# Raw modulation weights in a second buffer, and the pooling and convolution work of VectorE at other places in the mixer rounds

## What is computed

```python
def trunk_layer(x, cond, st, ...):
    mod = (jax.nn.silu(cond) @ ada_w + ada_b).astype(x.dtype).reshape(cond.shape[0], N_MOD, 1, D_MODEL)
    sh1, sc1, gt1, sh2, sc2, gt2 = [mod[:, i] for i in range(N_MOD)]
    h = rms_norm(x, norm_g[0]) * (1 + sc1) + sh1
    y, st = mixer_sublayer(h, st, w_in, ...)
    x = x + gt1 * rms_norm(y, norm_g[1])
    h = rms_norm(x, norm_g[2]) * (1 + sc2) + sh2
    a = dwconv_centred(h @ ffn_up, ffn_conv)
    val, gate = jnp.split(a, 2, axis=-1)
    y = (jax.nn.silu(gate) * val) @ ffn_down
    x = x + gt2 * rms_norm(y, norm_g[3])
    return x, st

def mixer_sublayer(h, st, w_in, ...):
    z = h @ w_in                       # q, k, v, o, gates g, gu, gv, pz, cb, cc, cx
    h_a, new_st = bi_mlstm(heads(q), heads(k) * (MLSTM_DH ** -0.5), heads(v), gates, st)
    y_a = jax.nn.sigmoid(o) * h_a
    y_b = chunk_spatial_gate(gu, gv, gmlp_ws, gmlp_b)
    y_c = multiscale_pool(pz, pool_w, pool_scale)
    y_d = cb * dwconv_centred(cc * cx, conv_w)
    return jnp.concatenate([y_a, y_b, y_c, y_d], axis=-1) @ w_out, new_st
```

## Time and profile before

| | before |
|---|---|
| median of 3 runs (lowest to highest) | 829.67 us (828.95 to 832.6) |
| the profiled execution, its own time | 826.83 us |
| its span, first to last instruction | 825.0 us |
| mean granted TensorE clock | 0.972 |
| busy: TensorE / VectorE / ScalarE / GpSimd | 765.9 / 470.8 / 315.6 / 85.8 us |

### The profile page before, as it was taken

One profiled execution on the slowest core, in us unless ns is written; L12 is line 12 of the kernel. 1 busy time (PEld: TensorE's weight loads), 2 busy tenths in 40 slices (PEclk: granted clock), 3 DMA queues, 4 the chain that ended last, 5 costly groups with the idle time before them and its releaser, 6 DMA issues.

```text
span 825.0 us, 12596 instructions
## 1 busy us (share of the span) xinstructions
PE 765.9 (93%) x4754; PEld 692.8 (84%) x4754; DVE 470.8 (57%) x743; ACT 315.6 (38%) x520; POOL 85.8 (10%) x125
## 2 busy tenths in 40 slices
PE   4799999979977998799999999999999999999996
PEld 2489898868866686599999999999999987878785
DVE  2651455755645559765564655555555656756754
ACT  5541422111112247753444335343433333326442
POOL 7600023121200261200000000000000000000000
PEclk9899999989988999899999999999999999999998
DMA  9953108464435854442222222213131235533561
GB/s 301 352 139 106 52 18 240 120 174 134 154 127 204 249 172 130 130 123 77 77 76 76 74 79 76 76 51 102 52 101 51 95 109 169 187 129 124 200 220 68
DMA packets 99534, 107.21 MB, mean 130 GB/s; under 512 B 7000, under 2 KB 79864, under 8 KB 99368
## 3 DMA queue, kind: packets, MB, share of 16 engines
q1 hardware_dynamic: 94007, 94.79, 37.1%
q0 software_dynamic: 3632, 10.20, 4.2%
q10 hardware_dynamic: 1856, 1.71, 0.7%
HBM read 103.89 MB, written 2.80 MB: 129 GB/s over the span
## 4 chain that ended last, share of the span: by engine, by line
PE 80%; DVE 8%; issue 4%; DMA 3%; ACT 3%; POOL 1%; SPq 0%; DVEq 0%; ACTq 0%; POOLq 0%
PE PAIR L1695 48%; PE PAIR L1886 22%; PE PAIR L1705 4%; DMA RAW<-in_w_in_dram 3%; PE PAIR L1684 2%; ACT WHI L892 1%; PE PAIR L1642 1%; DVE T L1538 1%; DVE WLO L1149 1%; DMA POSC<-in_pos_col_dram 1%; DVE X L1546 1%; PE PAIR L1659 1%; PE PAIR L1651 1%; ACT JUNK L1049 1%; DVE ASLO L1500 0%
## 5 line engine op out<-in xcount | busy, mean ns | idle before, releaser
L1695 PE MATMUL PAIR<-Hhi,WHI 128*128 128x320 f32 x928 | 220.5, 316 | 21.8 <-DVE MODROW L1184 14.3
L1695 PE MATMUL PAIR<-Hlo,WHI 128*128 128x320 f32 x928 | 217.7, 314 | 0.0
L1695 PE MATMUL PAIR<-Hhi,WLO 128*128 128x320 f32 x928 | 217.7, 313 | 0.0
L1695 PEld LDWEIGHTS PAIR<-Hhi,WHI 128*128 128x128 f32 x928 | 159.3, 192 | 25.0 <-DVE MODROW L1184 15.2
L1695 PEld LDWEIGHTS PAIR<-Hlo,WHI 128*128 128x128 f32 x928 | 159.6, 192 | 0.0
L1695 PEld LDWEIGHTS PAIR<-Hhi,WLO 128*128 128x128 f32 x928 | 159.2, 192 | 0.0
L1149 DVE TENSOR_TENSOR WLO<-RAW,WHI 128x1024 fp32r<-128x1024 f32 (+1 forms) x80 | 99.1, 1243 | 67.7 <-ACT WHI L892 57.9
L892 ACT ACTIVATE WHI<-RAW 128x1024 fp32r<-128x1024 f32 (+1 forms) x80 | 83.4, 1047 | 32.2 <-DMA RAW<-in_w_in_dram 27.6
L1886 PE MATMUL PAIR<-WHI,ASHI 128*128 128x512 f32 x282 | 90.2, 401 | 5.0 <-DVE ASLO L1500 3.5
L1100 ACT ACTIVATE UP<-PAIR 128x128 f32<-128x128 f32 x132 | 36.5, 350 | 139.8 <-PE PAIR L1695 139.8
L1886 PE MATMUL PAIR<-WHI,ASLO 128*128 128x512 f32 x282 | 88.9, 396 | 0.0
(11 more groups left out here) (243 smaller groups left out, 786.1 us busy)
## 6 DMA issues: line engine op xcount, KB each, us to landing
RAW<-in_ffn_up_dram SPq DMA_DIRECT2D x44, 512.0 KB, 3.7
RAW<-in_ffn_down_dram SPq DMA_DIRECT2D x44, 512.0 KB, 4.1
RAW<-in_ada_w_dram SPq DMA_DIRECT2D x32, 512.0 KB, 4.2
RAW<-in_w_in_dram SPq DMA_DIRECT2D x20, 512.0 KB, 4.9
RAW<-in_w_out_dram SPq DMA_DIRECT2D x16, 512.0 KB, 4.7
HALL<-in_ada_w_dram SPq DMA_DIRECT2D x10, 512.0 KB, 10.3
out_dram<-X SPq DMA_DIRECT2D x5, 512.0 KB, 5.6
WLOA<-in_ada_w_dram SPq DMA_DIRECT2D x4, 512.0 KB, 8.4
```

What stands on the lines that cost most here:

```text
L1695: last = pe.matmul(t[:, 512 * half:512 * half + HALF], w[:, n_or_slot, cols(k)], h[:, k, HALF * half:HALF * half + HALF], start=(k == 0 an ...
```

## The change

A raw unit whose slot predecessor is raw too is loaded into the low buffer instead (`WLOA` is `WLO` seen as plain float32), at the same slot number, with semaphores of its own (`lo_in`). The rule `lo_home` picks the second pieces of ad 5 to ad 11 (units 30, 33, 36, 39, 42, 45, 48), units 50 and 51 of ada 4 and units 56 and 57 of ada 5. A load then waits for the last user of its own buffer, and VectorE, before it writes the low part of a tile's unit, waits for the last raw piece in the slot (`wait_lo_home`). `pool_tile` is cut in two: the sums stay at `cc`, the edges and the combine stand at the beginning of VectorE's work for `cx`. The convolution's three operations move from `cb` to `pl`, which is ahead of the `prep` of the round of `cb`.

```diff
+        lo_home = [False] * NU
+        for n in range(HEAD_UNITS + RING, UP0):
+            m, raws = n - RING, ("ad", "ada")
+            lone = UNITS[n][:2] == ("ada", 4) and UNITS[n + RING][0] not in raws
+            lo_home[n] = UNITS[n][0] in raws and (lone or UNITS[m][0] in raws) and not lo_home[m]
+
         def raw_at(n, w=D):
-            return AREA[n][:, 0:w] if in_area(n) else RAW[:, n % RING, 0:w]
+            if in_area(n):
+                return AREA[n][:, 0:w]
+            return WLOA[:, n % RING, 0:w] if lo_home[n] else RAW[:, n % RING, 0:w]
...
+        def same_home_before(n, lo):
+
+            m = n - RING
+            while m >= HEAD_UNITS and lo_home[m] != lo:
+                m -= RING
+            return m
...
+        def wait_lo_home(eng, n):
+
+            m = same_home_before(n, True)
+            if m >= HEAD_UNITS:
+                eng.wait_ge(release[m][0], release[m][1])
+
...
             def wait_raw(n):
 
-                m = n - RING
+                if lo_home[n]:
+                    wait_slot(sp, n)
+                    wait_lo_home(sp, n)
+                    return
+                m = same_home_before(n, False)
                 if in_area(m):
                     return
...
                     dve.wait_ge(hi_split, splits_to[u + 1])
                     wait_slot(dve, u)
+                    wait_lo_home(dve, u)
...
                 elif kind == "cx":
 
+                    pool_edges(n)
                     t = wait_filled(dve, s)
...
                 elif kind == "cc":
-                    pool_tile(n)
-                elif kind == "cb":
+                    pool_sums(n)
+                elif kind == "pl":
                     wait_copied(dve, ("cx", n))
                     dve.wait_ge(pooled, n + 1)
...
                                              op0=ALU.mult, op1=ALU.add).then_inc(conv_done, 1)
+                elif kind == "cb":
                     t = wait_filled(dve, s)
                     dve.wait_ge(conv_done, n + 1)
```

More of the change, by code:

```diff
@@ L385, in hybrid_trunk_layer @@
         raw_in = [sem(f"raw_in{i}") for i in range(RING)]
+        lo_in = [sem(f"lo_in{i}") for i in range(RING)]
         area_in = [sem(f"area_in{i}") for i in range(HEAD_UNITS)]
@@ L470, in in_area @@
             return n < HEAD_UNITS
+        lo_home = [False] * NU
[3 more added lines that the diff above has]
+            lo_home[n] = UNITS[n][0] in raws and (lone or UNITS[m][0] in raws) and not lo_home[m]
         def raw_at(n, w=D):
-            return AREA[n][:, 0:w] if in_area(n) else RAW[:, n % RING, 0:w]
+            if in_area(n):
+                return AREA[n][:, 0:w]
+            return WLOA[:, n % RING, 0:w] if lo_home[n] else RAW[:, n % RING, 0:w]
         def raw_count(n):
-            return 16 * sum(2 if UNITS[m][0] == "vg" else 1 for m in range(n % RING, n + 1, RING) if not in_area(m))
+            return 16 * sum(2 if UNITS[m][0] == "vg" else 1 for m in range(n % RING, n + 1, RING)
+                            if not in_area(m) and lo_home[m] == lo_home[n])
         def wait_raw_in(eng, n):
@@ L481, in wait_raw_in @@
                 eng.wait_ge(area_in[n], 16)
+            elif lo_home[n]:
+                eng.wait_ge(lo_in[n % RING], raw_count(n))
             else:
                 eng.wait_ge(raw_in[n % RING], raw_count(n))
+        def same_home_before(n, lo):
[3 more added lines that the diff above has]
+            return m
         def width(n):
@@ L553, in hybrid_trunk_layer @@
             while n < NU and n < UPTO[key] + AHEAD:
-                r = release.get(slot_before(n)) if is_split(n) else None
-                if r is not None and (r[2] > at_ or r[2] == at_ and r[0] is not ada_used):
+                users = [release.get(m) for m in (slot_before(n), same_home_before(n, True))] if is_split(n) else []
+                if any(r is not None and (r[2] > at_ or r[2] == at_ and r[0] is not ada_used) for r in users):
                     break
@@ L651, in load @@
                 wait_raw(n)
+                if lo_home[n]:
+                    (o, a, b, src), = source(UNITS[n])
+                    sp.dma_start(raw_at(n).rearrange("p (a b) -> p a b", a=a), src).then_inc(lo_in[n % RING], 16)
+                    return
                 slot = RAW[:, n % RING, :]
@@ L1451, in output_gate, with pool_sums @@
                 dve.tensor_tensor(Y[:, n, :], TMP[n][:, :], t[:, 0:TOK], ALU.mult).then_inc(drained[USE[s][0]], 1)
-            def pool_tile(j):
+            def pool_sums(j):
                 wait_copied(dve, ("pz", j))
@@ L1470, in pool_tile, with pool_edges @@
                     link(dve.tensor_tensor(SCb[hi, a:b], SBb[hi, a - 4:b - 4], SBb[hi, a + 4:b + 4], ALU.add))
+            def pool_edges(j):
+                z = SA[:, 1, :]
+                lo, hi = slice(0, 64), slice(64, P)
                 for r, t in ((lo, SBb), (hi, SCb)):
```

## The result

| | before | after |
|---|---|---|
| median (lowest to highest), runs on one chip | 829.31 us (827.89 to 832.6), 4 runs | 806.12 us (804.45 to 806.92), 4 runs |
| the profiled execution, its own time | 826.83 us | 806.92 us |
| its span | 825.0 us | 805.1 us |
| mean granted TensorE clock | 0.972 | 0.980 |
| busy: TensorE / VectorE / ScalarE / GpSimd | 765.9 / 470.8 / 315.6 / 85.8 us | 759.4 / 474.1 / 315.9 / 85.6 us |

The changed kernel takes 0.9712 of the time (95% interval 0.968 to 0.9745), 23.2 us less by the medians. The profiled execution of the changed kernel is the longest of its four; that of the kernel before is shorter than all four of its runs.

A forecast was written before the change was run, and what follows sets the result against it. No engine was full: TensorE waited in the mixers for late loads and VectorE. Tile terms of 20.7 us less 0.5 for remaining waits gave 20.2, taking the 829.67 median to 809.5 us; range 806.5 to 817.5.

The forecast's parts named there:

- pz1: Fifth of ten mixer tiles; its late weight load would come earlier, removing 5.69 us of idle and 2.49 of slow clock.
- cx1: Seventh mixer tile, held up by VectorE's pool chain; 2.71 us of idle and 1.54 of slow clock would go.
- o0: Ninth mixer tile; its weight load would go out earlier, removing 4.20 us of idle and 2.40 of slow clock.
- cc0: Second mixer tile; its load would no longer share the way with another, removing 0.77 us of idle.
- cx0: Third mixer tile; the 0.91 us of TensorE idle ahead of it would go.
- o1: Tenth and last mixer tile; its load still waits for its raw slot, so 4.33 us of idle and slow start stay.
- Unit 40: Weight load of tile pz1; would go out 12.4 us earlier, ahead of the state outputs, and land within 7.5 us.
- rival 3: The in-order queue stops at another entry, loads come no earlier; only VectorE's moves gain, 5.4 us, time 824.3; chance 0.05.
- the clock terms: Tiles pz1, cx1 and o0 would no longer start at the 1.2 GHz level, gaining 2.49, 1.54 and 2.40 us.
- Rival 1: VectorE becomes the bound in the mixer rounds, 0.76 us in four and one slow tile; gain 15.2, time 814.5; chance 0.15.
- Rival 2: State outputs catch other loads or GpSimd's spreads, so pz1 or cc1 waits; gain 12.0 us, time 817.7; chance 0.08.
- rival 4: Slower: VectorE's row copy late in cc1, cx0, cx1 and cb1, 6.2 us each; time 833.8; chance 0.02.

## Why the prediction was right, and where it missed

**Right by its own steps.** Idle ahead of pz1, cx1, o0, cc0 and cx0: all gone, as the terms said. o1 gained nothing, and its cause, the raw slot held by unit 55, is shown by the kernel that frees that slot: 4.61 us of idle and 2.9 us of slow start went with it. Unit 40 goes ahead of the state outputs and lands after 5.1 us, within the 7.5 allowed. The stretch is 137.0 us long at 0.98 ("some 137", "0.97 or above"). The profiled execution took 806.92 us for the 806.6 of the sum, but that it came so close is luck: the mixers gave 1.0 us more than 20.2, and head and tail, which the sum did not touch, took 1.3 us more. The shares are right in their order: without VectorE's two moves 16.4 us, where the sum less rival 3's 5.4 leaves 14.8. VectorE's moves alone gave 5.8, for rival 3's 5.4; that this fits is partly luck too, since the moves also took 3.2 us of idle ahead of pz1, which rival 3 does not have.

**The terms, one by one.** Each tile that started late had been set against 7.30 us; a tile that nothing delays takes 7.04 (7.10 for cx1). That was worth 0.20 to 0.27 us at five tiles, 1.25 us in all. So the clock terms were too small: they measured a slow tile against one that had itself started after an idle time. The 0.5 us held back for remaining waits were not there: no tile but o1 waits at all. Against this o1 came out 0.9 us worse than before in this execution (4.61 and 10.03 us for 4.33 and 9.38). 20.7 + 1.25 − 0.9 is 21.0, and the mixers gave 21.2.

**The step that failed** is the last of the sum: "The median of before is 829.67, 2.8 above the profiled one; the same gain makes 809.5." It carried the distance of one profiled execution to its median over to the other kernel. There the median is not 2.8 us above the profiled execution but 0.8 us below it (806.12 and 806.92), and these 3.6 us are, within 0.3, the whole error. The profiled execution of before was not an ordinary one: of the three executions of before it has the shortest head, the shortest mixers and the shortest tail. The forecast is 3.4 us above the result, and the later runs say of what it is made. The median of three runs, 829.67, was 1.3 us above that of 73. The gain was 2.0 us larger than 20.2: 0.5 for waits that did not remain and 0.5 for the terms above (21.2 for 20.7), and the rest is what the mean of three pairs of executions has over the first pair: mixers of 149.6 instead of 148.8 us before and of 126.9 instead of 127.6 after (1.5 us, of which the medians, 22.2 apart, show 1.0). The changed kernel's first mixers were long by o1's slow start (its tile took 10.03 us, and 8.80 in the third execution). Before's are longer mainly because loads that are issued just in time land later than in the first profile (cx1's after 6.90 and 7.71 us, with idle of 3.63 and 4.43 instead of 2.71). That wait too is gone in all three profiles of the changed kernel. The changed kernel's times spread almost as widely as before's all the same (803.88 to 808.94 over 16 runs, 825.02 to 832.6 over 73), so late loads are not the main source of the spread between executions. The range named the difference between the medians, but reached down only 3.0 us from the forecast.

**The rivals.** Rival 1, VectorE becomes the bound: no. The longer convolution operation is seen, 1.52 us for 0.90, the third and not the first, but putting the convolution back changed nothing. (The prediction put the long first operation of the earlier trace rows down to GpSimd's issue of the spreads; it was the GpSimd operation behind that issue, as the last section shows.) Nor was all slack spent: in the tightest round, cc1, VectorE's copy of the row ends at 194.68, 0.26 us before the tile cx1 takes over in the chain at 194.94, where the prediction had 0.3. VectorE then waits 0.74 us more for the results of C:

```profile
194.27 0.41 DVE L1218 COPY MODROW<-PAIR 128x256 f32<-128x256 f32 x1
195.42 0.16 DVE L1417 SCALAR_TENSOR_TENSOR DEN<-PAIR,COLS 128x4 f32<-128x4 f32 x1 [0.74 <-PE PAIR L1889]
```

Rival 2, the outputs catch other loads: its mechanism is seen in full, the load of unit 43 with 20.3 us and prep5's spread with a wait of 2.49 us, but at the price of nothing. With the outputs moved away the wait was gone and the time the same. In the kernel before the same jam made TensorE wait 5.69 us in the one place and 5.09 us in the other. Rival 3 and rival 4: no, the loads came earlier and no row copy was late.

The Trainium skill's "DMA: Bandwidth & Descriptors" (Issuing engines are not separate DMA queues), by which DMAs of all issuing engines interleave on the same 16 engines, agrees with all the jams shown: 12.61, 17.73 and 20.3 us for loads on SyncE's queue beside outputs issued by ScalarE, 5.1 us for the one that went ahead.

## What to carry to other kernels

When raw data holds a slot that a split needs, look for a buffer of the same slot that lies idle meanwhile. Here no load with a round to spare made TensorE wait any more, whether it landed after 5.1 or 20.3 us and wherever the small outputs were sent, and the gain was larger than the idle time that the first profile showed, by the slow starts behind it. Once the loads are early, look again at what each of the reordered pieces is worth; here the cut in the pool chain carried 6.7 us and the moved convolution nothing. And before a gain of 20 us is put on a median, ask where the profiled execution stands among the runs: one profile and three runs left 3 us open. The distance of a profiled execution to its median belongs to that execution, and not to the kernel.

## What the runs showed of the hardware

- Operations of VectorE beside GpSimd: the third convolution operation took 1.52 us at 164.43 and 0.90 us where GpSimd did nothing. In the timeline of GpSimd a `TENSOR_TENSOR` of 0.63 us began 0.18 us after it, while the second convolution operation had only the issue of the spreads beside it and took its 0.90 us (VectorE's timeline, then GpSimd's):

```profile
163.49 0.90 DVE L1463 SCALAR_TENSOR_TENSOR SBb<-SA,SCOL,SBb 128x656 f32<-128x656 f32 x1
```
```profile
163.40 1.19 POOL L832 DMA_DIRECT2D WE<-weight_rows  x2 [2.57 <-issue]
164.61 0.63 POOL L854 TENSOR_TENSOR KW<-KT,COLS 128x256 f32<-128x256 f32 x1
```

  The excess, 0.62 us, is the length of that operation. It is there in both rounds of all three profiles of the changed kernel (1.50 to 1.52 us). The Trainium skill's "SBUF — State Buffer" (SBUF: two separate sides) says that a VectorE operation with two inputs in SBUF and a GpSimd operation that reads SBUF exclude each other for a whole instruction, and that the one that starts first goes ahead; the excess agrees with the first half, but by the trace VectorE had started first (GpSimd's times in a trace are rough). The first convolution operation, which the prediction feared for, took 0.56 us in its new place. Its 1.31 us of the earlier trace rows, from 224.95 on, had the same companion, 0.31 us behind its start:

```profile
225.26 0.63 POOL L821 TENSOR_TENSOR KW<-KT,COLS 128x256 f32<-128x256 f32 x1
```

- A load of 512 KB landed after 5.1 us ahead of the state outputs and after 20.3 us behind them; their packets are nearly all under 512 bytes. Without them the landing scatters less, but enough to matter when a load is issued just in time: in the kernel before cx0's load took 5.1, 6.61 and 8.34 us in three executions, cx1's 4.9, 6.90 and 7.71.
- The tail's scatter sits in one place. In all fourteen profiled executions the code behind the mixers is the same, and the tail took 549.8 to 553.6 us. Counted from the output projection's first matmul, the clock was 0.99 or 1.00 everywhere but from 50 to 100 us. There it was 0.93 in the two executions with a tail of 549.8 us, 0.90 in the three with 551.2 or 551.3, and 0.83 in the seven with 553.0 to 553.4; the two at 0.86 had 551.9 and 553.6, so the clock there does not tell all. These are the changed kernel with the outputs late (tail 549.8 us) and its third execution without an edit (553.4 us):

```profile
302.23:352.23 50.00, 41.89 (x254) 38.11 (x255) 36.60 (x53) 29.24 (x55) 6.72 (x7) 0.93 0.46 127
```
```profile
303.56:353.56 50.00, 41.27 (x229) 36.69 (x230) 34.50 (x50) 27.47 (x51) 6.71 (x7) 0.83 0.42 116
```

  In the same 50 us the second gets through 25 matmuls fewer. No edit here aimed at that scatter. Two profiled executions of the unchanged kernel before were 5.3 us apart, so a difference of a few microseconds between two profiled executions says nothing about the kernels by itself; the mixers alone, read from instruction to instruction, agreed within 1.7 us.
